# Prompt attention ahead of the mLSTM stages, and layer norms from running sums with raw rows in the up projection, in a one-core decoder layer

## The chip, the cores and the metric

The kernel runs on one core of a Trainium2 chip. The metric is the device time of one execution in microseconds (us), smaller is better. The engines are TensorE (PE), VectorE (DVE), ScalarE (ACT), GpSimd (POOL) and SyncE (SP), which here only issues transfers. Each runs its own program in order, and they meet through semaphores.

## The reference

One step of a hybrid decoder layer for 512 prompt tokens and 8 sequences of 4 sample tokens (544 columns, float32, width 1024):

```python
z = x @ w_in + b_in                      # 27 tiles of 128 features
qk = silu(causal_conv(m_qk)); h = mlstm_chunkwise(...)      # 8 heads of 64
mix_m = sigmoid(m_o) * head_norm(h)
mix_n = g0 * compressed + g1 * selected + g2 * window       # 8 query, 2 kv heads, each softmax + relative bias
x1 = layer_norm(ALPHA * x + concat(mix_m, mix_n) @ w_out, ln1_w, ln1_b)
u = causal_conv(x1 @ w_up + b_up, width 3)                  # 5376 features
y = layer_norm(ALPHA * x1 + (gelu(u[:2688]) * u[2688:]) @ w_down + b_down, ln2_w, ln2_b)
```

Also returned are new cache rows, windows, the mLSTM states and the last rows before each convolution. ALPHA is 2 ** 0.25. `layer_norm` takes mean and variance over the 1024 features of a token.

## The kernel before

Features lie on partitions, tokens in columns: KD = 8 tiles of 128 features and NT = 544 columns (T = 512 prompt, NS = 32 sample). Every dense projection is done in fp32r: weights and activations are each split into a high part (rounded) and a low part (the rest), and three products are summed for each k. `project` (L1653 to L1675) makes one output tile from `parts` weight items: for each k, three products of two matmuls (256 and 288 columns, L1667 and L1669), 48 matmuls for KD = 8.

Weights come as 74 items: 27 of w_in, 8 of w_out (`I_OUT` on), 42 of w_up (`I_UP` on) and 24 of w_down (`I_DOWN` on, 8 tiles in 3 parts of 7 k). SP loads item i into `wring` (4 slots) when item i-4 has been used (`load_weights`, L581 to L585). ACT copies it rounded into `whi` (2 slots) when item i-2 has been used (`split_hi`, L471 to L477; the copy itself is `high`, L466), and DVE makes the low part (`split_lo`, and `low`, L469). `w_hi`, `w_lo` and `w_used` count these steps. All splits stand in the ACT and DVE programs two items ahead of the matmuls.

The stages, in PE's order, all on the same core and with the order written out by hand in each engine's block:

1. In-projection (27 tiles), with the decode attention of the 8 sequences woven into it; then 60 transposes to token rows (L1951), to 308 us.
2. mLSTM for the prompt, four chunks of 128 tokens (PE from L1965), and the sample mLSTM (`sd_*` semaphores), to 412.
3. Pooling of compressed keys and values (L2089, L2090), then the prompt attention: 32 pairs of (block, branch, head) with scores, exponentials, transposes and values, PE two pairs ahead (`PAIRS`, `LAG`), `cmp_scores` and `cmp_transposed` (L2104, L2110) for the compressed branch. ACT and PE wait for `sd_end` 2 and for the copies of state outputs; `mixed` (L1549) writes the upper half of `mixt`.
4. Out projection, 8 tiles from `mixt` (`out_tile`), and with it `norm_pe` and `norm_dve`. After each tile DVE adds ALPHA times the input (L1585, L1588), and PE, in front of the tile after next, adds an average of these rows with a 1/1024 matrix (`average`, L2174 to L2176, two matmuls of float32).
5. Layer norm 1: subtract the mean (L1602, L1605), square on ACT (L989), average the squares on PE, square root (L991, L993), reciprocal of 544 columns (L1608), multiply (L1611), affine on ACT (L996), and splits of x1.
6. Up projection, 42 tiles. For tile n, DVE and ACT run, in this order:

```python
split_lo(dve, I_UP + n + 2)                     # DVE
dve.wait_ge(f_u, n + 1)
link(dve.tensor_scalar(t, u[:, 0:560], ...))    # L1635, first tap
link(dve.scalar_tensor_tensor(out=t, ...))      # L1636, second tap
dve.tensor_copy(fc[:, n, 0:2], u[:, 512:514])   # L1638, and L1639: last rows
dve.scalar_tensor_tensor(out=t, ...).then_inc(f_conv, 1)   # L1640, third tap
# every second tile: gate(n // 2 - 1), gated_lo(n // 2 - 2)

split_hi(act, I_UP + n + 2)                     # ACT
act.activation(us[:, :, 0:2], hf[:, n, :], ACT.Copy)       # L1023
act.activation(u[:, 2:514], q4[n % 2], ACT.Identity, bias=vec("b_up", n))   # L1024, PSUM to SBUF
act.activation(us[:, :, 2:6], ...).then_inc(f_u, 1)        # L1026
# every second tile: gelu(n // 2), gated_hi(n // 2 - 1)
```

   PE may write tile n when `f_u` says that tile n-2 has been read. `gate` (L1627, L1628) multiplies the two halves; `link` orders an operation behind the one before it on the same engine by a semaphore.
7. Down projection, 8 tiles of 3 items (`down_tile`), evicted by ACT into `ybuf` (L1041, L1043), added on DVE (L1597, L1598), averaged as in 4; then layer norm 2 with the same code, and the output.

The SP queue takes, behind the in-projection: the table of biases `relrow` (L611), its shifted form `tb` (L615, 2 MB), the mLSTM states, w_out items 0 to 3, state outputs, the window copy `out_win_s` (L635, 4 MB, memory to memory), the history `hf` of the ffn convolution (L636), the reload of x into `xt` (8 transfers), then all weight items that are left.

## Time and profile before

| | us |
|---|---|
| three runs | 1025.5, 1032.95, 1031.28 |
| median | 1031.28 |
| profiled execution | 1037.76 |
| its span | 1036.1 |
| PE busy | 917.0 (89%) |
| DVE busy | 517.5 (50%) |
| ACT busy | 374.2 (36%) |
| POOL busy | 99.3 (10%) |
| mean granted clock | 0.896 |

The span is the time between the first and the last instruction of one profiled execution, and 1.7 us lie outside it. Busy shares are means over stages that differ. PEclk is the granted clock of TensorE as a share of 2.4 GHz. A matmul that starts while its predecessor runs has a duration that overlaps it; what counts in the projections is the distance from start to start.

### The profile page before, as it was taken

Reading aid. Unit: us, or ns where it says so; the run is one execution under the profiler, and the core shown is the slowest. Engines: PE = TensorE matmul, PEld = TensorE weight load, DVE = VectorE, ACT = ScalarE, POOL = GpSimd, SP = SyncE. Lnnn points to the kernel's source line nnn. Section 1 sums busy time; section 2 is a strip of 40 time slices with the busy share of each in tenths; the row PEclk is TensorE's granted clock in tenths of the full one; section 3 lists DMA queues with packets and bytes.
Section 4 is the critical chain, followed back from the end, with each engine's and each line's share of the span. In section 5 each row is a group of like instructions: output and inputs, shape, how many; then the busy total and the mean of one; then the engine's idle time right before and its main releaser. Section 6 shows DMA issues by size and latency. Waiting matters only on the chain.

```text
span 1036.1 us, 19860 instructions
## 1 busy us (share of the span) xinstructions
PE 917.0 (89%) x7903; PEld 821.8 (79%) x7903; DVE 517.5 (50%) x1116; ACT 374.2 (36%) x742; POOL 99.3 (10%) x164
## 2 busy tenths in 40 slices
PE   5999988998898667888869959999999999999993
PEld 5888877787776553655559839999999999999992
DVE  4522345522335566566752265766776677332325
ACT  4322344644421010345651155434433443222115
POOL 1012213343341002000000000000000000000000
PEclk9989999899896555569989969999999999999997
DMA  8247777676462001400022202222222222222212
GB/s 292 70 145 256 229 264 235 207 223 180 127 233 89 6 1 42 175 1 1 2 87 82 82 1 75 89 82 85 100 82 82 95 90 72 89 90 76 86 33 87
DMA packets 53152, 112.46 MB, mean 109 GB/s; under 512 B 6954, under 2 KB 30283, under 8 KB 52611
## 3 DMA queue, kind: packets, MB, share of 16 engines
q1 hardware_dynamic: 45648, 91.68, 25.9%
q0 software_dynamic: 6528, 17.83, 5.4%
q10 hardware_dynamic: 882, 1.67, 0.5%
q8 instruction: 63, 1.03, 0.4%
q14 instruction: 31, 0.25, 0.1%
HBM read 105.54 MB, written 12.40 MB: 114 GB/s over the span
## 4 chain that ended last, share of the span: by engine, by line
PE 80%; DVE 9%; ACT 4%; issue 3%; DMA 3%; ACTq 0%; POOLq 0%; POOL 0%; SPq 0%; DVEq 0%
PE q L1669 30%; PE q L1667 27%; PE q L2114 3%; DMA arena<-in_pool 2%; PE q L2142 2%; PE q L2132 2%; PE q L1731 1%; PE q L2175 1%; PE q L2176 1%; PE q L2002 1%; PE q L2056 1%; PE q L1719 1%; PE q L1785 1%; ACT whi L956 1%; PE q L1965 1%
## 5 line engine op out<-in xcount | busy, mean ns | idle before, releaser
L469 DVE TENSOR_TENSOR wring_r<-wring,whi_r 128x1024 fp32r<-128x1024 f32 (+1 forms) x101 | 120.5, 1194 | 341.8 <-ACT whi_r L466 341.7
L466 ACT ACTIVATE whi_r<-wring 128x1024 fp32r<-128x1024 f32 (+1 forms) x101 | 104.2, 1033 | 327.8 <-PE q L1669 316.9
L1669 PE MATMUL q<-xt_r,whi_r 128*128 128x288 f32 x552 | 166.9, 302 | 0.0
L1667 PE MATMUL q<-xt_r,whi_r 128*128 128x256 f32 x552 | 157.5, 285 | 0.0
L1667 PE MATMUL q<-arena_r,whi_r 128*128 128x256 f32 x440 | 137.6, 313 | 19.6 <-DVE xt_r L469 11.5
L1669 PE MATMUL q<-arena_r,whi_r 128*128 128x288 f32 x440 | 133.7, 304 | 0.0
L1669 PE MATMUL q<-arena_r,wring_r 128*128 128x288 f32 x440 | 133.0, 302 | 0.0
L1667 PE MATMUL q<-arena_r,wring_r 128*128 128x256 f32 x440 | 125.9, 286 | 0.0
L1667 PE MATMUL q<-mixt_r,whi_r 128*128 128x256 f32 x400 | 113.2, 283 | 10.5 <-DVE xt_r L469 10.5
L1669 PE MATMUL q<-mixt_r,whi_r 128*128 128x288 f32 x400 | 119.4, 298 | 0.0
L1667 PEld LDWEIGHTS q<-arena_r,whi_r 128*128 128x128 f32 x440 | 86.2, 196 | 27.4 <-issue 19.7
L1667 PEld LDWEIGHTS q<-xt_r,whi_r 128*128 128x128 f32 x552 | 107.0, 194 | 0.0
L1669 PEld LDWEIGHTS q<-xt_r,whi_r 128*128 128x128 f32 x552 | 106.8, 193 | 0.0
L1669 PE MATMUL q<-mixt_r,wring_r 128*128 128x288 f32 x336 | 100.1, 298 | 0.0
L1667 PE MATMUL q<-mixt_r,wring_r 128*128 128x256 f32 x336 | 94.5, 281 | 0.0
L1669 PEld LDWEIGHTS q<-arena_r,whi_r 128*128 128x128 f32 x440 | 86.5, 197 | 0.6
L1667 PEld LDWEIGHTS q<-arena_r,wring_r 128*128 128x128 f32 x440 | 85.8, 195 | 0.0
L1669 PEld LDWEIGHTS q<-arena_r,wring_r 128*128 128x128 f32 x440 | 85.4, 194 | 0.0
L1667 PEld LDWEIGHTS q<-mixt_r,whi_r 128*128 128x128 f32 x400 | 76.2, 190 | 11.0 <-issue 10.9
L1669 PEld LDWEIGHTS q<-mixt_r,whi_r 128*128 128x128 f32 x400 | 76.0, 190 | 0.0
L1667 PEld LDWEIGHTS q<-mixt_r,wring_r 128*128 128x128 f32 x336 | 63.6, 189 | 0.0
L1669 PEld LDWEIGHTS q<-mixt_r,wring_r 128*128 128x128 f32 x336 | 63.5, 189 | 0.0
(406 smaller groups left out, 1584.1 us busy)
## 6 DMA issues: line engine op xcount, KB each, us to landing
wring<-in_w_up SPq DMA_DIRECT2D x42, 512.0 KB, 3.2
wring<-in_w_in SPq DMA_DIRECT2D x27, 512.0 KB, 5.1
arena<-in_pool SPq DMA_DIRECT2D x64, 192.0 KB, 3.1
arena<-in_pool POOLq DMA_DIRECT2D x64, 192.0 KB, 3.9
wring<-in_w_down SPq DMA_DIRECT2D x24, 448.0 KB, 3.1
arena<-in_pool SPq DMA_DIRECT2D x64, 64.0 KB, 2.1
arena<-in_pool POOLq DMA_DIRECT2D x64, 64.0 KB, 2.4
wring<-in_w_out SPq DMA_DIRECT2D x8, 512.0 KB, 7.3
```

Of the source, the lines that this page charges most:

```text
L466: return eng.activation(out, src, ACT.Copy)
L469: return eng.tensor_tensor(out, src, hi.bitcast(F32), ALU.subtract)
L956: act.activation(ptb[:, m % 2, g, 0:w], bank[4 + g][:, 0:w], ACT.Copy).then_inc(np_te, 1)
L1667: pe.matmul(out[:, 0, 0:HALF], w, x[:, 0:HALF], start=(kk == 0 and n == 0), stop=(end and n == 2))
L1669: mm = pe.matmul(out[:, 1, 0:HALF + NS], w, x[:, HALF:NT], start=(kk == 0 and n == 0), stop=(end and n == 2))
L1719: mm = pe.transpose(t[:, 128 * k:128 * k + 128], on_chip(g, i, k)[:, 256:384], ident)
L1731: mm = pe.matmul(bank[4][32 * k:32 * k + 32, 128 * s + 64 * e:128 * s + 64 * e + 64], wslide[:, e, h, 12 - 4 * u:44 - 4 * u], pg, start=(i ...
L1785: return pe.matmul(bank[7][ROWS * s:ROWS * s + ROWS, 0:128], probs[:, ROWS * s:ROWS * s + ROWS], v, start=start, stop=stop, skip_group_che ...
L1965: mm = pe.matmul(bank[q], gl[:, token_rows(c)], rows[:, c % 2, 512 * q:512 * q + 512], start=True, stop=True)
L2114: return pe.matmul(bank[6][p, 128 * j:128 * j + 128], v, probs, start=start, stop=stop, skip_group_check=True)
L2132: mm = pe.matmul(bank[2 * (m % 2) + g][:, 0:w], q_of(GQ * g + j, i), zt[64 * g:64 * g + 64, (Z_SK, Z_WK)[k], 0:w], start=True, stop=True)
L2142: mm = pe.transpose(bank[4 + g][:, 128 * kk:128 * kk + 128], pb[:, m % 3, g, 128 * kk:128 * kk + 128], ident)
```

## The change

Two things at once.

Order: the pooling and the prompt attention come directly behind the token transposes, and the mLSTM for the prompt waits for the attention's last block (`np_mx`). Buffers that both used have been moved apart. The first broadcast of the table goes from SP to ACT's queue, at in-projection tile 22; `tb` is loaded in two transfers, columns 384 to 511 first (`tb_in`), the rest (`tb_rest`) awaited by the scores of block 1. The reload of x goes ahead of the sample mLSTM's outputs; `hf` goes ahead of the window copy, and both go ahead of w_out items 4 to 7, at the start of the out projection. The rows of w_out are reordered so that the attention half comes first, and that half of `mixt` is split before the mLSTM ends; behind it DVE makes four low parts, then the low part of w_out item 0.

Norms: in the out projection only tile 0's mean is taken on PE (`first_mean`, inside tile 1), and 8 times it is subtracted from all rows as `shift`. DVE keeps a running `total` of the tiles and a sum of `squares` (squared on ACT). The rows as they are, times ln1_w, are split (`raw_hi` on ACT, `raw_low` on DVE) and go straight into the up projection, with two more columns, ln1_w and ln1_b, in each product (290 columns for 288). Mean and variance are found while it runs: `means` behind k 4 of up tile 0 (averages, and token sums in 5 columns), `variance` and `inverse` on 5 columns, `spread` (back to 544 columns) behind k 2 of tile 1. Each up tile is then corrected from PSUM by DVE (`scaled_rows`), copied by ACT into `u`, and ACT makes the first tap; the copies of the last rows go to POOL. In the down projection DVE rebuilds ALPHA times x1 (`residual`, four or five linked operations) and adds the product from PSUM; `ybuf` is gone, as are the averages behind each tile. The last tile is added to precomputed averages.

```diff
-            sp.wait_ge(rel_out, 16)
-            sp.dma_start(relrow.ap(), relone.ap().unsqueeze(1).broadcast_to([H, 128, NREL])).then_inc(rel_out, 16)
             sp.wait_ge(rel_out, 32)
             sp.wait_ge(nd_mx, GROUPS)
-            shifted = bass.AP(tensor=relrow, offset=127, ap=[[NREL - 1, 128], [128 * NREL, H], [1, 512]])
-            sp.dma_start(tb, shifted).then_inc(tb_in, 16)
+            def shifted_table(first, n):
+                return bass.AP(tensor=relrow, offset=127 + first, ap=[[NREL - 1, 128], [128 * NREL, H], [1, n]])
+            sp.dma_start(tb[:, :, 384:512], shifted_table(384, 128)).then_inc(tb_in, 16)
+            sp.dma_start(tb[:, :, 0:384], shifted_table(0, 384)).then_inc(tb_rest, 16)
             sp.dma_start(ctv, a["ct"]).then_inc(sd_in, 16)
             sp.dma_start(ntv, a["nt"]).then_inc(sd_in, 16)
             sp.wait_ge(w_used, ZT)
-            sp.dma_start(n0, a["n0"]).then_inc(sd_in, 16)
             for i in range(I_OUT, I_OUT + RING):
                 load_weights(i)
+            sp.wait_ge(np_mx, QT)
+            sp.dma_start(n0, a["n0"]).then_inc(sd_in, 16)
             sp.wait_ge(ml_ce, QT)
             sp.dma_start(a["out_c_p"], carried[:, QT % 2]).then_inc(st_cp, 16)
+            sp.wait_ge(ml_mx, 4)
...
             sp.wait_ge(sd_end, 2)
             sp.wait_ge(st_cs, 16)
+            sp.dma_start(hf, a["hf"]).then_inc(hist, 16)
             sp.wait_ge(stored, 64)
             sp.dma_start(a["out_win_s"], a["win"][:, TS:, :]).then_inc(stored, 16)
-            sp.dma_start(hf, a["hf"]).then_inc(hist, 16)
-            sp.wait_ge(np_mx, QT)
-            for k in range(KD):
-                sp.dma_start(xt[:, k, :], a["xt"][:, k, :]).then_inc(xin2, 16)
             for i in range(I_OUT + RING, len(ITEMS)):
...
+            for n in range(UP):
+                pool.wait_ge(f_u, n + 1)
+                pool.tensor_copy(fc[:, n, 0:2], uf[:, n % 4, 512:514])
+                pool.tensor_copy(fc[:, n, 2:18].rearrange("p (b t) -> p b t", b=NB),
+                                 by_sequence(uf, n, 6)[:, :, 4:6]).then_inc(f_last, 1)
...
+                    act.wait_ge(f_last, n - 3)
...
+                act.wait_ge(rw_u, n + 1)
+                act.activation(u[:, 2:514], t[:, 0:T], ACT.Identity, bias=b, scale=-1.0)
+                act.activation(us[:, :, 2:6], t[:, T:NT].rearrange("p (b t) -> p b t", b=NB), ACT.Identity,
+                               bias=b, scale=-1.0).then_inc(f_u, 1)
+                act.wait_ge(f_u, n + 1)
+                act.activation(tf[:, n % 4, 0:560], u[:, 0:560], ACT.Identity, bias=vec("fconv_b", n),
+                               scale=vec("fconv_w", n)).then_inc(f_one, 1)
...
+            def residual(base, m):
+                t = xt[:, m, :]
+                if base == 0:
+                    if m == 0:
+                        dve.wait_ge(xin2, 16 * KD)
+                    else:
+                        link(dve.scalar_tensor_tensor(out=t, in0=t, scalar=ALPHA, in1=shift, op0=ALU.mult, op1=ALU.subtract))
+                else:
+                    link(dve.tensor_tensor(t, raw_lo[:, m, 0:NT].bitcast(F32), raw_hi[:, m, 0:NT].bitcast(F32), ALU.add))
+                    link(dve.tensor_tensor(t, t, rstd, ALU.mult))
+                    link(dve.scalar_tensor_tensor(out=t, in0=mean, scalar=vec("ln1_w", m), in1=t, op0=ALU.mult,
+                                                  op1=ALU.subtract))
+                    link(dve.tensor_scalar(t, t, -ALPHA, var[:, m:m + 1], ALU.mult, ALU.add))
+                    if m >= 1:
+                        link(dve.tensor_tensor(t, t, shift, ALU.subtract))
+            def added(base, m):
+                dve.wait_ge(w_used, I_OUT + m + 1 if base == 0 else I_DOWN + DOWN_PARTS * (m + 1))
+                t = xt[:, m, :]
+                t2, p = t[:, 0:T].rearrange("p (c t) -> p c t", c=2), q4[m % 2]
+                if base == 0 and m == 0:
+                    dve.scalar_tensor_tensor(out=t2, in0=t2, scalar=ALPHA, in1=p[:, :, 0:HALF], op0=ALU.mult, op1=ALU.add)
+                    dve.scalar_tensor_tensor(out=t[:, T:NT], in0=t[:, T:NT], scalar=ALPHA, in1=p[:, 1, HALF:HALF + NS],
+                                             op0=ALU.mult, op1=ALU.add).then_inc(ln_d, 1)
+                else:
+                    dve.tensor_tensor(t2, t2, p[:, :, 0:HALF], ALU.add)
+                    dve.tensor_tensor(t[:, T:NT], t[:, T:NT], p[:, 1, HALF:HALF + NS], ALU.add).then_inc(ln_d, 1)
+            def first_shifted(base):
+                dve.wait_ge(ln_act, act_stat(base // KD, "shift"))
+                dve.wait_ge(ln_d, unshifted(base // KD))
+                dve.tensor_tensor(xt[:, 0, :], xt[:, 0, :], shift, ALU.subtract).then_inc(ln_d, 1)
+                dve.wait_ge(ln_d, shifted_rows(base // KD, 0))
+            def sums(base, m):
+                dve.wait_ge(ln_d, shifted_rows(base // KD, m))
+                link(dve.tensor_tensor(total, total, xt[:, m, :], ALU.add))
+            def sums_of_squares(base, m):
+                dve.wait_ge(ln_q, base + m + 1)
+                dve.tensor_tensor(squares, squares, sq_m, ALU.add).then_inc(ln_a, 1)
+                dve.wait_ge(ln_a, (KD - 1) * (base // KD) + m)
+            def raw_low(m):
+                dve.wait_ge(rw_hi, m + 1 if m == 0 else m + 2)
+                dve.scalar_tensor_tensor(out=raw_lo[:, m, 0:NT], in0=xt[:, m, :], scalar=vec("ln1_w", m),
+                                         in1=raw_hi[:, m, 0:NT].bitcast(F32), op0=ALU.mult,
+                                         op1=ALU.subtract).then_inc(rw_lo, 1)
...
+                residual(0, m)
+                added(0, m)
+                split_lo(dve, I_OUT + m + 2)
                 if m >= 1:
+                    sums(0, m)
+                    sums_of_squares(0, m)
+                    raw_low(m)
...
+            def scaled_rows(n):
+                p, t = q4[n % 2], scaled[n % 2]
+                dve.wait_ge(w_used, I_UP + n + 1)
+                if n == 0:
+                    dve.wait_ge(ln_act, act_stat(0, "copied"))
+                if n >= 2:
+                    dve.wait_ge(f_u, n - 1)
+                c1 = p[:, 1, HALF + NS:HALF + NS + 1]
+                dve.tensor_scalar(rowsum[:, n % 2:n % 2 + 1], p[:, 1, HALF + NS + 1:HALF + NS + 2], vec("b_up", n), None,
+                                  ALU.add)
+                dve.scalar_tensor_tensor(out=t[:, 0:T].rearrange("p (c t) -> p c t", c=2),
+                                         in0=mean[:, 0:T].rearrange("p (c t) -> p c t", c=2), scalar=c1,
+                                         in1=p[:, :, 0:HALF], op0=ALU.mult, op1=ALU.subtract)
+                link(dve.scalar_tensor_tensor(out=t[:, T:NT], in0=mean[:, T:NT], scalar=c1,
+                                              in1=p[:, 1, HALF:HALF + NS], op0=ALU.mult, op1=ALU.subtract))
+                dve.tensor_tensor(t, t, rstd, ALU.mult).then_inc(rw_u, 1)
             for n in range(UP):
+                if n == 0:
+                    variance(0)
+                    inverse(0)
                 split_lo(dve, I_UP + n + 2)
-                dve.wait_ge(f_u, n + 1)
+                scaled_rows(n)
+                dve.wait_ge(f_one, n + 1)
                 u, t = uf[:, n % 4, :], tf[:, n % 4, 0:560]
-                link(dve.tensor_scalar(t, u[:, 0:560], vec("fconv_w", n), vec("fconv_b", n), ALU.mult, ALU.add))
                 link(dve.scalar_tensor_tensor(out=t, in0=u[:, 1:561], scalar=vec("fconv_w", UP + n),
                                               in1=t, op0=ALU.mult, op1=ALU.add))
-                dve.tensor_copy(fc[:, n, 0:2], u[:, 512:514])
-                dve.tensor_copy(fc[:, n, 2:18].rearrange("p (b t) -> p b t", b=NB), by_sequence(uf, n, 6)[:, :, 4:6])
                 dve.scalar_tensor_tensor(out=t, in0=u[:, 2:562], scalar=vec("fconv_w", 2 * UP + n),
                                          in1=t, op0=ALU.mult, op1=ALU.add).then_inc(f_conv, 1)
...
+            dve.wait_ge(ln_pe, pe_stat(1, "mean"))
+            centred(0)
+            variance(1)
+            centred(1)
+            inverse(1)
+            for m in range(2, KD):
+                centred(m)
+            dve.wait_ge(ln_pe, pe_stat(1, "spread"))
+            for m in range(KD):
...
+            def first_mean(n):
+                pe.wait_ge(ln_d, unshifted(n))
+                average(xt[:, 0, :], q4[2]).then_inc(ln_pe, 1)
...
+            def means():
+                pe.wait_ge(ln_a, KD - 1)
+                token_means(total, bank[6])
+                average(total, q4[2]).then_inc(ln_pe, 1)
+                token_means(squares, bank[7]).then_inc(ln_pe, 1)
+            def spread(n):
+                pe.wait_ge(ln_dve, 2 * n + 2)
+                pe.matmul(bank[6], ones, scaled[0][:, 0:T], start=True, stop=True)
+                pe.matmul(bank[7][:, 0:NS], ones, scaled[0][:, T:NT], start=True, stop=True).then_inc(ln_pe, 1)
...
+            pe.wait_ge(sd_end, 2)
+            for m in range(KD):
+                out_tile(m)
             for n in range(UP):
-                if n >= 2:
+                if n < 2:
+                    pe.wait_ge(ln_d, shifted_rows(0, KD - 2 + n))
+                else:
                     pe.wait_ge(f_u, n - 1)
-                project(q4[n % 2], I_UP + n, 1, by_k(x1_hi), by_k(xt_lo), KD, y_lo if n == 0 else None)
-            norm_pe(KD, down_tile)
+                project(q4[n % 2], I_UP + n, 1, by_k(raw_hi), by_k(raw_lo), KD, rw_lo if n == 0 else None,
+                        {0: [(4, means, ())], 1: [(2, spread, (0,))]}.get(n, ()), NT + 2)
+            for m in range(KD):
+                down_tile(m)
+            pe.wait_ge(ln_a, 2 * KD - 3)
+            average(total, q4[2], last=False)
+            token_means(total, bank[6], last=False)
+            token_means(squares, bank[7], last=False)
+            pe.wait_ge(ln_d, shifted_rows(1, KD - 1))
+            average(xt[:, KD - 1, :], q4[2], first=False).then_inc(ln_pe, 1)
+            token_means(xt[:, KD - 1, :], bank[6], first=False)
+            pe.wait_ge(ln_q, 2 * KD)
+            token_means(sq_m, bank[7], first=False).then_inc(ln_pe, 1)
+            spread(1)
```

## Rows read from the trace of the kernel before

**Rows 1.** The page, chain that ended last: share of the span by engine.

```profile
PE 80%; DVE 9%; ACT 4%; issue 3%; DMA 3%; ACTq 0%; POOLq 0%; POOL 0%; SPq 0%; DVEq 0%
PE q L1669 30%; PE q L1667 27%; PE q L2114 3%; DMA arena<-in_pool 2%; PE q L2142 2%; PE q L2132 2%; PE q L1731 1%; PE q L2175 1%; PE q L2176 1%; PE q L2002 1%; PE q L2056 1%; PE q L1719 1%; PE q L1785 1%; ACT whi L956 1%; PE q L1965 1%
```

**Rows 2.** Windows: us, busy PE, PEld, DVE, ACT, POOL, PEclk, DMA share, GB/s.

```profile
308.60:412.50 103.90, 75.77 (x503) 57.00 (x505) 62.31 (x120) 9.71 (x12) 11.43 (x9) 0.55 0.10 39
...
412.50:462.00 49.50, 43.16 (x246) 29.94 (x246) 26.71 (x141) 20.08 (x84) 0.00 (x0) 0.53 0.25 101
462.00:532.10 70.10, 57.98 (x517) 38.05 (x515) 45.27 (x159) 42.85 (x120) 0.00 (x0) 0.97 0.00 1
...
536.40:592.00 55.60, 55.60 (x408) 54.66 (x409) 17.73 (x28) 9.54 (x11) 0.00 (x0) 0.96 0.27 93
592.00:619.20 27.20, 12.88 (x43) 8.34 (x41) 17.10 (x30) 13.54 (x20) 0.00 (x0) 0.76 0.06 20
619.20:875.00 255.80, 255.80 (x2018) 255.69 (x2019) 172.63 (x312) 107.61 (x213) 0.00 (x0) 0.99 0.25 84
875.00:1007.00 132.00, 132.00 (x1032) 131.05 (x1031) 39.05 (x46) 29.70 (x43) 0.00 (x0) 1.00 0.24 77
1007.00:1036.10 29.10, 11.90 (x42) 7.96 (x41) 15.84 (x27) 14.22 (x21) 0.00 (x0) 0.76 0.20 78
```

**Rows 3.** Timeline, PE at the attention's start: start, us, operation, [idle before <-releaser].

```profile
421.95 0.48 PE L2110 MATMUL q<-cst,xt 128*128 128x128 f32 x1 [2.60 <-DVE xt L1522]
```

**Rows 4.** Timeline, PE from the last out tile to the first up tile.

```profile
592.01 0.59 PE L2175 MATMUL q<-xt,cst 128*128 128x256 f32 x2
...
595.33 0.91 PE L2175 MATMUL q<-xt,cst 128*128 128x256 f32 x2 [2.24 <-DVE xt L1588]
...
619.19 0.55 PE L1667 MATMUL q<-mixt_r,whi_r 128*128 128x256 f32 x1 [10.51 <-DVE xt_r L469]
```

**Rows 5.** Timeline, ACT's weight splits: one in out, one in up.

```profile
564.64 1.06 ACT L466 ACTIVATE whi_r<-wring 128x1024 fp32r<-128x1024 f32 x1 [5.85 <-PE q L1669]
...
627.44 1.06 ACT L466 ACTIVATE whi_r<-wring 128x1024 fp32r<-128x1024 f32 x1 [1.96 <-PE q L1669]
```

**Rows 6.** Timeline of SP's queue, and transfers: count, KB each, us to landing.

```profile
414.89 0.77 SPq L635 DMA_DIRECT2D out_win_s<-in_win  x1
...
smem<-in_hf SPq DMA_DIRECT2D x1, 336.0 KB, 22.5
...
wring<-in_w_out SPq DMA_DIRECT2D x8, 512.0 KB, 7.3
...
wring<-in_w_up SPq DMA_DIRECT2D x42, 512.0 KB, 3.2
```

**Rows 7.** Timeline, DVE in one up tile with a gate.

```profile
797.62 1.23 DVE L469 TENSOR_TENSOR wring_r<-wring,whi_r 128x1024 fp32r<-128x1024 f32 x1 [2.50 <-ACT whi_r L466]
798.77 0.57 DVE L1635 TENSOR_SCALAR smem<-zt,col 128x560 f32<-128x560 f32 x1
799.37 0.80 DVE L1636 SCALAR_TENSOR_TENSOR smem<-zt,col,smem 128x560 f32<-128x560 f32 x1
...
801.07 0.68 DVE L1627 TENSOR_TENSOR zt<-smem 128x512 f32<-128x512 f32 x1
...
801.77 0.72 DVE L469 TENSOR_TENSOR zt_r<-zt,arena_r 128x544 fp32r<-128x544 f32 x1
```

**Rows 8.** Timeline, ACT in one up tile.

```profile
791.56 0.67 ACT L1024 ACTIVATE zt<-q,col 128x512 f32<-128x512 f32 x1
792.13 0.28 ACT L1026 ACTIVATE zt<-q,col 128x32 f32<-128x32 f32 x1
792.30 0.67 ACT L1011 ACTIVATE smem<-smem 128x560 f32<-128x560 f32 x1
```

**Rows 9.** Groups by form: ACT's affine of the norms (busy, mean ns, idle).

```profile
L996 ACT ACTIVATE xt<-xt,col 128x544 f32<-128x544 f32 x16 | 12.6, 827 | 8.8 <-DVE xt L1611 8.8
```

**Rows 10.** Timeline, the second norm's reciprocal and affine.

```profile
1023.00 3.55 DVE L1608 RECIPROCAL smem<-smem 128x544 f32<-128x544 f32 x1 [6.42 <-ACT smem L993]
...
1027.35 5.96 ACT L996 ACTIVATE xt<-xt,col 128x544 f32<-128x544 f32 x8 [4.38 <-DVE xt L1611]
```

More of the change, by code:

```diff
@@ L227, in layer @@
         xt, zt, wring, whi_f, mixt, arena = (sb(*t) for t in large("", F32))
+        raw_lo, work = xt_r, xt[:, :, :].rearrange("p k c -> p (k c)")
+        xt_r, xt = (t[:, :, 0:NT] for t in (xt_r, xt))
         cst = sb("cst", [128, NC128])
@@ new lines, in gated @@
+            def gated(m):
+                i, k, j, slot = m // 8, m // 4 % 2, m % 4, m % 3
+                dve.wait_ge(np_e, NG * m + 2)
+                link(dve.reciprocal(dens[:, 4 + slot, :], dens[:, slot, :]))
+                for g in range(NG):
+                    v, gate = pb[:, slot, g, 0:128 * i + 128], 104 + 24 * i + 8 * k + GQ * g + j
+                    dve.tensor_scalar(v, v, dens[:, 4 + slot, g:g + 1], gcol[:, gate:gate + 1],
+                                      ALU.mult, ALU.mult).then_inc(np_p, 1)
@@ L1306, in _ @@
+            mixed(QT - 1)
             rescale = s4[:, 16:32]
```

679 lines of the change are left out of this document (360 added, 319 removed).

## The prediction

> **What bounds the kernel now.** I read the chain of waits first: TensorE holds 80% of it, and two matmul lines alone 57% [rows 1]. The windows by stage come next [rows 2]. The reader is to see three kinds of stage in them. In the out, up and down projections PE is busy for the whole stretch (55.6, 255.8 and 132 us). In the two layer norms (592 to 619.2 and 1007 to 1036.1) it is busy for 12.9 and 11.9 us of 27.2 and 29.1. In mLSTM and prompt attention no engine is full, and the clock is 0.55 and 0.53 until 462, so a hand-over chain sets the pace. The change touches all three. The first norm is nearly pure delay, and it goes; but its work goes to the up stage, where DVE is busy for 172.6 of 255.8 us, or 4.11 us of each 6.09 us tile. So the question is what VectorE and ScalarE need per tile afterwards.
>
> The sum is made against the profiled execution, 1037.76 us (span 1036.1 and 1.7 around it); it is 6.5 us above the median of 1031.28, which I take off again at the end. Less than 1% (10 us) can't be told from no change here.
>
> **Swap of attention and mLSTM: -2.** Both stages stand in series before and after, with the same instructions, and only the first sees another state of the clock. The stretches of 103.9 and of 119.6 us (49.5 and 70.1) are laid in the other order [rows 2]. The attention waits for its table of biases, but columns 384 to 511, all that block 0 reads, are loaded ahead of the other three quarters, and those are wanted at block 1 only. So no wait shows there. The gain could be in the clock: the first 49.5 us of attention run at 0.53 (1.2 GHz), with DVE busy for 26.7 (54%), against 65% (45.27 of 70.1) later at 0.97. At that share they would take 26.7/0.65 = 41, 8 us less. But attention has a hole of 2.60 us just behind its start [rows 3], and a hole of 2.24 us in the norm was followed by matmuls at half speed (0.91 us per pair against 0.59) [rows 4]. I take -2, with bounds of -10 (the clock stays up, and mLSTM's start gets some of it too) and +3 (mLSTM's first 10 us slower). Splitting the attention half of the mix early leaves 3.9 us between the last mLSTM product and the first out tile, about the 4.3 of before.
>
> **Out projection: -4.3, +1.5.** Before, one average of 0.87 us stands behind each tile, so a weight split of 1.06 comes after 5.85 idle, every 6.91 us [rows 5], instead of 6.04. Now it is 8 x 6.04 + 2.1 slow start + 0.87 for the one first average = 51.3, against 55.6. DVE has two more 544-column additions, a subtraction and a raw low part: 1.14 + 0.7 + 4 x 0.72 = 4.8 us a tile, which TensorE's 6.04 hides (if it were not hidden: nothing up to 6.04, then 1 for 1).
> The 4 MB window copy now goes into SP's queue ahead of w_out tiles 4 to 7, and every load behind it waits. Before it was issued 3 us after the mLSTM stage, and what was queued behind it took 22.5 us to land [rows 6]. Now: 3 + 0.8 + 22.5 = 26.3, then a weight tile, 3.2 us if it is like the up loads, 7.3 like the out loads: tile 4 lands at 29.5 to 33.6. TensorE would start it at 3.9 + 2.1 + 0.87 + 4 x 6.04 = 31.0, and the two splits before that take 2.3, so it is late from 28.7 on, by 0.8 to 4.9. I take +1.5, since the copy will have the queues for itself; bounds 0 and 7.1 (4.9 and a slow restart of 2.2: the first up tile took 8.2 us from 619.19 to 627.44 for 6.01 [rows 4, 5]).
>
> **First norm: -27.2.** Raw rows split behind each out tile are ready when the last tile ends: for the last of them, product 7 of the first up tile, the low part comes 4.5 us after it and is wanted after 7 x 0.75 = 5.3. The hole of 2.24, the average and the 3.55 us reciprocal on 544 columns go from the path. The whole 27.2 us window goes [rows 2]. Bounds -27.2 and -25 (the row sum late once).
>
> **Up projection: +41.4.** TensorE's own time stays near 6.04 (290 columns for 288, under 0.02 each) plus the token means, 2.8, and spread, 0.95, in the first two tiles: 260.5. But VectorE is now in a round trip with ScalarE inside each tile. One iteration, in its program order, from rows of DVE and ACT in one old tile [rows 7, 8]:
> - weight low part: 1.14 to the next start (797.62 to 798.77).
> - row sum 0.08, scaled residual 0.60 (801.07 to 801.77 holds the same pair, 512 and 32 columns, as 0.60 and 0.10), 32 columns 0.21, times rstd 0.73: 1.62.
> - ACT's copy into u 0.57, the 32 columns 0.28, then the first tap with scale and bias. The trace has no 560-column one; for 544 with a scale and bias column it shows 827 ns [rows 9], for 560 without them 0.67. I take 0.85. With three hand-overs of 0.03: 1.79. In all of it VectorE stands, as every later operation of its program, gates and low parts too, waits behind this one; ScalarE's next weight split stands behind its wait for the scaled rows.
> - two taps: 0.84 + 0.71 (799.37 and its partner; linked steps start 0.03 after the end of the one before, free ones 0.08 before it).
> Sum 6.10. Even tiles add a gate and a low part, 1.33 (801.07 to the end of 801.77), so 7.43. After odd ones ScalarE does gelu, gated high part and weight split (0.58 + 0.57 + 1.06 less overlap = 2.15) while VectorE is ready after 1.58: +0.57. A pair is 6.10 + 7.43 + 0.57 = 14.1, 7.05 a tile against 6.04. VectorE's first u comes at 15.7; 15.7 + 20 x 14.1 = 297.7, so the stage is about 297.2: +41.4. TensorE gets holes of about 0.65 and 1.4 us per pair. Bounds: a tap of 0.67 gives 290 (+34); ScalarE never late gives 13.53 a pair, 286 (+30); links that cost nothing, 0.6 less a tile, 272 (+16); at 7.3 a tile 308 (+52). The copies of the last columns to POOL cost nothing: POOL has none busy in this stage [rows 2], and what waits on them is four tiles on.
> The Trainium skill speaks for a shorter cycle: "VectorE: DVE Perf Modes", section "The DRAIN you can't avoid", says that a semaphore between two operations costs nothing extra. The rows here differ: linked operations stand 0.12 us later than free ones. By the rule the stage would take the 272 of the last bound.
>
> **Down projection: +4.** Seven averages go (7 x 0.87 = 6.1, of which 5.2 lie in the stage) and one comes: -4.4. But VectorE ends the up stage late: after the last tile's taps it has a gate, two low parts, the prelude of the norm and a five-link residual before the third split. From the stage's start: 3.9 for what is left of tile 40 (taps, gate, low part), 6.1 for tile 41, 1.3 for the last gelu and gate, 1.4 for two low parts, 1.0 for the prelude, 3.2 for the residual and its links: that split ends at 16.9, and part 2 wants it after two parts of 5.3 (7 x 0.755), at 10.6. So +6.3, with a restart of 2.1 on top of -4.4. 132 becomes 136. Bounds -4.4 and +8.
>
> **Second norm: -6.3.** Averages of 544 columns and the reciprocal (3.55) [rows 10] become five-column ones: last value added 1.0, average 3.7, token sums 5.6, variance, root and inverse 8.3, subtractions 13.1, eight multiplies of 0.7 from PSUM 18.8, last ScalarE affine 19.9, and 2.8 from there to the end as before (1033.3 to 1036.1): 22.7 for 29.05. Bounds -9 and -3.
>
> **Sum.** -2 -4.3 +1.5 -27.2 +41.4 +4 -6.3 = +7.1: 1044.9 for the profiled execution, 1038.4 against the median, 0.7% above it. The gain of 38 us in the norms and averages is given back in the up stage.
>
> **The rivals.**
> (1) The up stage stays bound by TensorE, 260.5, and VectorE isn't late in down: -2 -4.3 +1.5 -27.2 +4.7 -4.4 -6.3 = -38: 993. For it: VectorE's own steps are (14.1 - 0.57 - 2 x 1.79) / 2 = 5.0 us of 6.04. Against it: the 1.79 us round trip stands in its program order, with no second tile's work between. 0.07.
> (2) Smaller: a faster cycle, 6.8 a tile (links or tap cheaper), and the clock up in the first attention: 297.2 - 42 x 0.25 = 286.7, +30.9 instead of +41.4, so 1027.9; with -8 for -2 as well, 1021.9. If links cost nothing at all, it is 272, +16, so 1013: 0.04 of this chance. (That is the time by the rule of the Trainium skill named above.) For: bounds above. Against: the measured links. 0.20.
> (3) Slower: the window copy ahead of w_out tile 4. It decides if that tile lands later than 28.7 us after the mLSTM stage; at 33.6 the price is 4.9 + 2.2 instead of 1.5: 1044.0. For: all out loads before took 7.3. Against: those stood in a crowd of other transfers. 0.15.
> (4) Short holes lower the clock again and again in the up stage. A restart costs 2.2 us [rows 4, 5]; in each of 21 pairs it would be mostly absorbed in the 2.05 us that TensorE has to spare: +4, 1042.5, and more if it never recovers (8.2 a tile: 1086). For it: the hole of 2.24 us. Against it: these holes, 0.65 and 1.4, are shorter than that one. The Trainium skill has a rule for it: "TensorE: Matmul & The Clock Gate", section "A second HAM failure mode: psum-queue depth-cycling", by which frequent short gaps between groups make the clock swing. 0.12.
> (5) Each hand-over is dearer than I take it, 7.3 a tile: +10.5, 1049. 0.12.
> (6) My forecast, 0.34, its own range 1028 to 1048.
>
> **Numbers.** Faster by over 1% (below 1021): (1) and 0.11 of (2) and 0.03 of mine, 0.21. Slower (above 1041.6): (3), (4), most of (5), 0.03 of mine, less 0.06 of them that ends nearer: 0.36. Within: 0.43. The range from 1015 to 1054 leaves out (1), the end of (2) and the tails of (4) and (5), 0.17 in all.
>
> **What would show it.** Up stage of about 297 us with PE busy share near 0.87, DVE intervals of 7.05 a tile, its idle time put down to ACT's first tap; no hole between out and up; out stage near 51 to 53; ACT's tap near 0.85; the tail 23 us behind the last down tile; w_out tile 4 landing near 29.5. Wrong, if DVE idles for TensorE in the up stage (then 993), or if the granted clock there is below 0.95.

## The result, and the profile after

The changed kernel takes 1048.87 us (median of 4 runs, 1048.64 to 1051.07) against 1032.12 for the kernel before (4 runs, 1025.5 to 1033.49): ratio 1.0181, 95% interval 1.0151 to 1.0211. I had forecast 1038.4, 0.7% above the median, which I counted as no change. The time lies inside the range of 1015 to 1054, but the loss is 1.8%, it can be measured, and it is more than twice what was forecast.

The chain that ended last, after:

```profile
PE 50%; DVE 23%; ACT 13%; issue 9%; DMA 3%; POOL 0%; SPq 0%; ACTq 0%; DVEq 0%; POOLq 0%
PE q L1837 15%; PE q L1835 15%; DVE cst L1764 3%; DMA arena<-in_pool 3%; ACT zt L1082 3%; DVE wring_r L493 3%; DVE cst L1759 3%; ACT whi_r L490 2%; PE q L2155 2%; ACT smem L1086 2%; PE q L2173 2%; DVE smem L1774 2%; PE q L2183 2%; PE q L1899 2%; PE q L2262 1%
```

TensorE had 80% of it and the two projection lines 57% [rows 1]; now they have 50% and 30%, and DVE and ACT hold 36% between them, with the lines of the up stage (L1764 times rstd, L1082 copy into u, L1086 first tap, L1774 second tap).

Windows by stage after (us, busy PE, PEld, DVE, ACT, POOL, PEclk, DMA share, GB/s), to be read beside [rows 2]. The stages are attention, mLSTM, out, up, down and the second norm:

```profile
306.60:418.90 112.30, 94.45 (x741) 61.85 (x741) 71.93 (x299) 61.56 (x200) 0.57 (x1) 0.85 0.01 4
418.90:526.40 107.50, 74.88 (x488) 56.59 (x489) 67.58 (x128) 15.62 (x22) 13.79 (x11) 0.56 0.10 35
526.40:577.70 51.30, 51.29 (x389) 51.14 (x390) 36.92 (x56) 17.44 (x26) 0.10 (x1) 0.95 0.42 155
577.70:885.00 307.30, 270.31 (x2046) 260.66 (x2044) 211.74 (x353) 142.77 (x253) 12.80 (x81) 1.00 0.22 72
885.00:1021.65 136.65, 130.08 (x1013) 129.57 (x1014) 75.94 (x108) 31.32 (x40) 0.55 (x4) 0.98 0.24 74
1021.65:1046.80 25.15, 10.31 (x54) 8.74 (x52) 14.01 (x40) 8.40 (x12) 0.00 (x0) 0.59 0.23 89
```

Up is the only stage that got much longer: 307.3 us for 255.8. TensorE is busy in it for 270.3, at a granted clock of 1.00, and DVE for 211.7, which is no full engine either. What it waits for stands in two views of the trace. First PE in two neighbouring tiles, then the waits of PE and of DVE in this stage (waiter, releaser: us in total, times, longest):

```profile
622.35 0.39 PE L1835 MATMUL q<-arena_r,whi_r 128*128 128x256 f32 x1 [0.54 <-ACT zt L1083]
630.07 0.39 PE L1835 MATMUL q<-arena_r,whi_r 128*128 128x256 f32 x1 [1.35 <-ACT zt L1083]
```

```profile
PE q L1835 <- ACT zt L1083: 36.9, 39, 1.4
...
DVE smem L1774 <- ACT smem L1086: 75.7, 40, 1.9
DVE wring_r L493 <- ACT whi_r L490: 10.9, 22, 1.5
```

PE has holes of 0.54 and 1.35 us in each pair of tiles, put down to ACT's copy into u, since that frees the PSUM bank. But ACT itself waits for DVE, and DVE stands 40 times for 1.9 us until ACT's first tap is done. So one chain goes back and forth between the two. One pair of it, on DVE and then on ACT:

```profile
660.13 0.80 DVE L1774 SCALAR_TENSOR_TENSOR smem<-zt,col,smem 128x560 f32<-128x560 f32 x1 [1.89 <-ACT smem L1086]
660.97 0.80 DVE L1776 SCALAR_TENSOR_TENSOR smem<-zt,col,smem 128x560 f32<-128x560 f32 x1
662.19 1.23 DVE L493 TENSOR_TENSOR wring_r<-wring,whi_r 128x1024 fp32r<-128x1024 f32 x1 [0.41 <-ACT whi_r L490]
663.33 0.21 DVE L1757 TENSOR_SCALAR sm<-q,col 128x1 f32<-128x1 f32 x1
663.46 0.74 DVE L1759 SCALAR_TENSOR_TENSOR cst<-dsc,q 128x512 f32<-128x512 f32 x1
664.12 0.24 DVE L1762 SCALAR_TENSOR_TENSOR cst<-dsc,q 128x32 f32<-128x32 f32 x1
664.40 0.72 DVE L1764 TENSOR_TENSOR cst<-cst,dsc 128x544 f32<-128x544 f32 x1
667.02 0.80 DVE L1774 SCALAR_TENSOR_TENSOR smem<-zt,col,smem 128x560 f32<-128x560 f32 x1 [1.89 <-ACT smem L1086]
...
674.73 0.80 DVE L1774 SCALAR_TENSOR_TENSOR smem<-zt,col,smem 128x560 f32<-128x560 f32 x1 [1.89 <-ACT smem L1086]
```

```profile
665.16 0.72 ACT L1082 ACTIVATE zt<-cst,sm 128x512 f32<-128x512 f32 x1 [2.90 <-DVE cst L1764]
665.79 0.31 ACT L1083 ACTIVATE zt<-cst,sm 128x32 f32<-128x32 f32 x1
666.13 0.86 ACT L1086 ACTIVATE smem<-zt,col 128x560 f32<-128x560 f32 x1
```

It is the chain of the prediction, step for step, only longer: 6.89 us from 660.13 to 667.02 and 7.71 to 674.73, 14.60 a pair for the 14.1 forecast.

The stages from first matmul to first matmul, of the two traces:

| stage | before | forecast | after | change |
|---|---|---|---|---|
| in-projection, to the transposes | 300.45 | 0 | 296.64 | -3.8 |
| transposes, attention, mLSTM, splits | 235.9 | -2 | 229.8 | -6.1 |
| out projection and first norm | 82.8 | -30.0 | 51.3 | -31.5 |
| up | 255.6 | +41.4 | 307.3 | +51.7 |
| down | 132.3 | +4 | 136.6 | +4.3 |
| second norm | 29.0 | -6.3 | 25.15 | -3.9 |
| span | 1036.1 | +7.1 | 1046.8 | +10.7 |

The first line is chance: in the eleven traces of this study the transposes start anywhere from 294.0 to 300.45, in either order of the stages, and the first trace of the kernel before is the latest. That is most of why its profiled execution stood 6.5 us above its median, while the changed kernel's (1048.81) lies at its median (1048.87). Taking 6.5 off was right.

### The profile page after: what moved, and what is told of

It reads as the page before. It is cut to its first block, busy times and chain, and to the rows that moved or that the text cites. A ratio compares the mean times of both kernels' runs of the same rounds, so it can differ in the third digit from the quotient of the medians.

```text
span 1046.8 us, 20115 instructions
## 1 busy us (share of the span) xinstructions
PE 901.9 (86%) x7863; PEld 806.2 (77%) x7863; DVE 595.6 (57%) x1233; ACT 400.1 (38%) x767; POOL 112.6 (11%) x248
## 4 chain that ended last, share of the span: by engine, by line
PE 50%; DVE 23%; ACT 13%; issue 9%; DMA 3%; POOL 0%; SPq 0%; ACTq 0%; DVEq 0%; POOLq 0%
PE q L1837 15%; PE q L1835 15%; DVE cst L1764 3%; DMA arena<-in_pool 3%; ACT zt L1082 3%; DVE wring_r L493 3%; DVE cst L1759 3%; ACT whi_r L490 2%; PE q L2155 2%; ACT smem L1086 2%; PE q L2173 2%; DVE smem L1774 2%; PE q L2183 2%; PE q L1899 2%; PE q L2262 1%
## 5 line engine op out<-in xcount | busy, mean ns | idle before, releaser
L1835 PE MATMUL q<-arena_r,whi_r 128*128 128x256 f32 x712 | 216.1, 304 | 62.9 <-ACT zt L1083 36.6
L1837 PE MATMUL q<-arena_r,whi_r 128*128 128x288 f32 (+1 forms) x712 | 214.0, 301 | 0.0
L1837 PE MATMUL q<-arena_r,wring_r 128*128 128x288 f32 (+1 forms) x712 | 213.1, 299 | 0.0
L1835 PE MATMUL q<-arena_r,wring_r 128*128 128x256 f32 x712 | 202.5, 284 | 0.0
L1835 PEld LDWEIGHTS q<-arena_r,whi_r 128*128 128x128 f32 x712 | 137.3, 193 | 78.6 <-ACT zt L1083 45.2
L1837 PE MATMUL q<-xt_r,whi_r 128*128 128x290 f32 (+1 forms) x552 | 165.5, 300 | 0.0
L1837 PEld LDWEIGHTS q<-arena_r,whi_r 128*128 128x128 f32 x712 | 137.7, 193 | 0.1
L1835 PEld LDWEIGHTS q<-arena_r,wring_r 128*128 128x128 f32 x712 | 137.0, 192 | 0.0
L1837 PEld LDWEIGHTS q<-arena_r,wring_r 128*128 128x128 f32 x712 | 136.7, 192 | 0.0
L1082 ACT ACTIVATE zt<-cst,sm 128x512 f32<-128x512 f32 x42 | 30.3, 722 | 159.2 <-DVE cst L1764 159.2
L1774 DVE SCALAR_TENSOR_TENSOR smem<-zt,col,smem 128x560 f32<-128x560 f32 x42 | 33.7, 802 | 79.5 <-ACT smem L1086 79.5
L1837 PE MATMUL q<-zt_r,whi_r 128*128 128x288 f32 x176 | 52.3, 299 | 0.0
L1835 PE MATMUL q<-zt_r,whi_r 128*128 128x256 f32 x176 | 49.4, 282 | 0.0
L965 ACT ACTIVATE xt<-xt 128x128 f32<-128x128 f32 (+3 forms) x64 | 35.4, 554 | 28.2 <-DVE xt L1410 27.8
```

Of the source, the lines that this page charges most:

```text
L965: act.activation(v, v, ACT.Exp, bias=mxs[:, 4 + slot, g:g + 1], accum_out=dens[:, slot, g:g + 1]).then_inc(np_e, 1)
L1082: act.activation(u[:, 2:514], t[:, 0:T], ACT.Identity, bias=b, scale=-1.0)
L1774: link(dve.scalar_tensor_tensor(out=t, in0=u[:, 1:561], scalar=vec("fconv_w", UP + n), in1=t, op0=ALU.mult, op1=ALU.add))
L1835: pe.matmul(out[:, 0, 0:HALF], w, x[:, 0:HALF], start=(kk == 0 and n == 0), stop=(end and n == 2))
L1837: mm = pe.matmul(out[:, 1, 0:width - HALF], w, x[:, HALF:width], start=(kk == 0 and n == 0), stop=(end and n == 2))
```

## The experiments

Theory A: in the up stage VectorE and ScalarE hand each tile back and forth, and what VectorE could do meanwhile stands behind the wait in its program. The rivals are VectorE's work as such, the clock, and the swap.

**The kernel before, again.**

> The kernel before, unchanged, for a second trace. Theory A (the clock of the first 50 us of attention is chance): its profiled execution is not at 1037.8 again but 4 to 12 us shorter, and the difference lies in the attention stage (119.6 us in the first trace) or in the in-projection (300.5 us). Theory B (the order sets the clock): 1035 to 1038 us again, attention at 119 to 120 us with a granted clock of 0.53 in its first 50 us.

Measured, in one run: 1031.88 us, span 1030.2, so 5.9 us less than the first trace's 1036.1. PE, start of the transposes and of the out projection:

```profile
295.62 6.63 PE L1951 MATMUL q<-cst,zt 128*128 128x128 f32 x54 [1.20 <-DVE zt L1081]
...
530.39 0.55 PE L1667 MATMUL q<-arena_r,whi_r 128*128 128x256 f32 x1 [4.28 <-DVE mixt_r L469]
```

The transposes start 4.8 us earlier, so most of the difference is in the in-projection. From transposes to out it is 234.8 us, against 235.9 in the first trace, and the first 49 us of attention have a granted clock of 0.57, against 0.53: attention is about as slow again. Theory A was right of the place it named second, B of the attention.

**The swap alone.**

```diff
# the kernel before, with the changed kernel's order of the stages, its buffers,
# its transfers (table, x, hf, window copy) and the early split of the mix; old norms
-            pe.wait_ge(np_mx, QT)
+            pe.wait_ge(sd_end, 2)
             norm_pe(0, out_tile)
```

> Only the swap of attention and mLSTM, with the buffers, queues and early splits that go with it; the norms, the up and the down projection stay as before. Theory B (the order keeps the clock up in attention, and the table's transfer is out of the in-projection's way): the -10 us that the trace of the changed kernel shows between the start and the out projection is real, so ratio 0.990, about 1022. Theory A (the first trace of before was a slow one in these stages): the ratio is 0.996 to 1.0, about 1029 to 1032, and the changed kernel's loss of 17 us against the median is the norms' alone.

Measured: 1030.59 us (12 runs) against 1031.24 (23 runs), ratio 0.9999 (0.9982 to 1.0016). From transposes to out its trace has 232.15 us, 2.6 less than the second trace of before, while the out projection and its norm take 0.2 and the second norm 0.5 more. So the swap is worth at most 2 us (the interval is -1.9 to +1.6 us), no more than what was forecast (-2), and the loss belongs to the norms. The 229.8 of the changed kernel's trace is at the low end: this trace and six others with the new order have 231.2 to 232.2, one has 229.2.

**The first tap back on VectorE.**

```diff
-                act.wait_ge(f_u, n + 1)
-                act.activation(tf[:, n % 4, 0:560], u[:, 0:560], ACT.Identity, bias=vec("fconv_b", n),
-                               scale=vec("fconv_w", n)).then_inc(f_one, 1)
...
-                dve.wait_ge(f_one, n + 1)
+                dve.wait_ge(f_u, n + 1)
+                link(dve.tensor_scalar(t, u[:, 0:560], vec("fconv_w", n), vec("fconv_b", n), ALU.mult, ALU.add))
```

> The changed kernel with the first convolution tap back on VectorE, behind f_u. Theory A (the round trip sets the up stage): VectorE stands only for 1.0 us (0.03 + 0.63 + 0.31 + 0.03) instead of 1.89, and does 0.60 more itself; ScalarE is no longer late after odd tiles. 6.1 and 7.45 a tile for 6.89 and 7.71, so a pair takes 13.5 for 14.6: the up stage takes 284 for 307, the whole 1026. Theory B (VectorE's work as such sets it, the stand is hidden by something): VectorE has 42 x 0.6 = 25 us more work, and the whole gets 10 to 25 us longer, 1059 to 1074.

Measured: 1029.7 us, ratio 0.9983 (0.9964 to 1.0002), 19 us less than the changed kernel. The up stage is 286.2 us (284 expected), with more work on VectorE, 233.2 us busy for 211.7:

```profile
581.50:867.70 286.20, 265.60 (x2045) 260.31 (x2044) 233.19 (x394) 110.60 (x212) 24.21 (x82) 1.00 0.24 77
```

```profile
664.56 0.57 DVE L1771 TENSOR_SCALAR smem<-zt,col 128x560 f32<-128x560 f32 x1 [1.00 <-ACT zt L1083]
```

The stand is 1.00 for 1.89. More work on the engine in the chain, and a shorter time: it is the round trip that costs, not the work. Theory B falls.

**The weight low part behind the scaled rows.**

```diff
-                split_lo(dve, I_UP + n + 2)
+                if n == 0:
+                    split_lo(dve, I_UP + n + 2)
                 scaled_rows(n)
+                if n >= 1:
+                    split_lo(dve, I_UP + n + 2)
                 dve.wait_ge(f_one, n + 1)
```

> The changed kernel with the weight low part of tile n+2 moved from ahead of the scaled rows of tile n to behind them (from tile 1 on): the same instructions, another order on VectorE. Theory A (the stand in the round trip is the cost): the low part of 1.14 lies in the 1.89 us stand, VectorE needs 1.79 + 1.89 + 1.55 = 5.2 in odd and 6.6 in even tiles, 5.9 on average, and TensorE's 6.04 sets the stage: 262 us for 307, the whole 1004, below the kernel before. Theory B (the sum of VectorE's work and hand-overs, whatever the order): no change, 1046 to 1050. Theory C (short holes throttle the clock): the stage stays above 280 with a granted clock below 0.95.

Measured: 1000.75 us, ratio 0.9702 (0.9675 to 0.973). The up stage takes 260.2 us. Its window, with nearly the same busy time on VectorE, then VectorE in one tile:

```profile
581.00:841.00 260.00, 259.93 (x2044) 259.07 (x2043) 213.55 (x356) 147.91 (x253) 13.04 (x82) 1.00 0.26 85
```

```profile
665.89 0.73 DVE L1764 TENSOR_TENSOR cst<-cst,dsc 128x544 f32<-128x544 f32 x1
666.53 1.22 DVE L493 TENSOR_TENSOR wring_r<-wring,whi_r 128x1024 fp32r<-128x1024 f32 x1
668.51 0.80 DVE L1777 SCALAR_TENSOR_TENSOR smem<-zt,col,smem 128x560 f32<-128x560 f32 x1 [0.76 <-ACT smem L1086]
```

The low part lies in the stand, which shrinks from 1.89 to 0.76, and PE is busy for 259.9 of 260.0 us. The down stage takes 132.3 us for 136.6, since VectorE comes less late to it: TensorE's hole in down tile 0, 6.57 us in the changed kernel, is 2.62 us here. This is one instruction in another place of the program, with the same work on each engine, and it is worth 48 us. It makes the change a gain.

**Half of it.**

```diff
-                split_lo(dve, I_UP + n + 2)
+                if n % 2 == 0:
+                    split_lo(dve, I_UP + n + 2)
                 scaled_rows(n)
+                if n % 2 == 1:
+                    split_lo(dve, I_UP + n + 2)
```

> The changed kernel with the weight low part behind the scaled rows in odd tiles only, half of the order that took the whole loss away. Theory A (the cycle of VectorE and ScalarE sets the stage until TensorE does): the 1.14 us go from one of the two tiles of a pair, 14.61 becomes 13.47, the up stage 283 for 307 and the whole 1025. Theory B (it is a matter of either or: one late tile in a pair keeps the stage at its old pace): 300 us or more in the up stage, 1040 or more.

Measured: 1026.14 us, ratio 0.9965 (0.9941 to 0.9988); the up stage 284.8 us for 283 expected. Half of the edit gives 22.5 of its 47.1 us, as in a chain that nothing else bounds yet.

**Two links more.**

```diff
-                dve.tensor_scalar(rowsum[:, n % 2:n % 2 + 1], ...)
-                dve.scalar_tensor_tensor(out=t[:, 0:T], ...)
+                link(dve.tensor_scalar(rowsum[:, n % 2:n % 2 + 1], ...))
+                link(dve.scalar_tensor_tensor(out=t[:, 0:T], ...))
```

> The changed kernel with two links more in each tile's scaled rows on VectorE: the row sum and the 512-column step are each waited for before the next step starts, which nothing needs. Theory A (a link between two VectorE operations costs 0.12 us on the engine that sets the stage, as linked steps start 0.03 to 0.04 behind the end and free ones 0.08 before it): 42 x 2 x 0.12 = 10 us more, 1059. Theory B (a semaphore between two VectorE operations costs nothing, the rule of the Trainium skill that was weighed in the prediction): no change, 1047 to 1051.

Measured: 1062.59 us, ratio 1.0317 (1.0292 to 1.0342). The up stage takes 317.7 us, 10.4 more than 307.3; 10.4 / 84 = 0.12 us a link. DVE, the row sum and the step behind it:

```profile
677.55 0.21 DVE L1757 TENSOR_SCALAR sm<-q,col 128x1 f32<-128x1 f32 x1
677.80 0.75 DVE L1759 SCALAR_TENSOR_TENSOR cst<-dsc,q 128x512 f32<-128x512 f32 x1
```

The distance is 0.25 for the 0.13 of 663.33 to 663.46. The other 3 to 4 us of the whole lie ahead of the up stage (it starts at 581.4 for 577.7), in the parts that vary. So a semaphore between two VectorE steps isn't free where that engine is in the chain. The Trainium skill's rule from the prediction ("VectorE: DVE Perf Modes", section "The DRAIN you can't avoid"), which it took from eight tensor copies, doesn't hold for these steps: the measurement is 0.12 us a link. The same section of the Trainium skill says that a next operation that is not held starts earlier, and there the trace agrees: in the changed kernel, without the link, the 512-column step starts 0.08 us before the recorded end of the row sum.

**Other operands.**

```diff
-                c1 = p[:, 1, HALF + NS:HALF + NS + 1]
+                c1 = vec("ln1_w", 0)
...
-                act.activation(u[:, 2:514], t[:, 0:T], ACT.Identity, bias=b, scale=-1.0)
+                act.activation(u[:, 2:514], t[:, 0:T], ACT.Identity, bias=b)
```

> The changed kernel with two operands changed, so that part of the computation is left out: the scaled rows take their factor from a constant column in SBUF and not from the product's own column in PSUM, and ScalarE's copy into u goes without the scale of -1. It measures what made the two steps longer than forecast. If the PSUM factor costs, the 512-column step of VectorE takes 0.68 (as the 512-column steps of before) and not 0.74; if the scale costs, ScalarE's copy takes 0.67 and not 0.72. If neither, both stay, and it is the source (two tensors from different memories on VectorE, SBUF in place of PSUM on ScalarE) that makes them longer.

Measured, in one run: 1049.8 us, up stage 307.0. Groups by form of the changed kernel, then of this one (busy, mean ns):

```profile
L1759 DVE SCALAR_TENSOR_TENSOR cst<-dsc,q 128x512 f32<-128x512 f32 x42 | 31.2, 742 | 0.0
...
L1082 ACT ACTIVATE zt<-cst,sm 128x512 f32<-128x512 f32 x42 | 30.3, 722 | 159.2 <-DVE cst L1764 159.2
```

```profile
L1759 DVE SCALAR_TENSOR_TENSOR cst<-dsc,col,q 128x512 f32<-128x512 f32 x42 | 31.0, 737 | 0.0
...
L1082 ACT ACTIVATE zt<-cst,sm 128x512 f32<-128x512 f32 x42 | 30.3, 723 | 158.8 <-DVE cst L1764 158.8
```

Neither the place of the factor (PSUM or SBUF) nor ScalarE's scale makes the steps longer than the rows that they were estimated from. For VectorE the traces show what does: that the factor is a column, one value for each partition, wherever it lies. The kernel before has the same kind of step with a constant as factor (ALPHA), and it too reads one tensor in SBUF and one in PSUM; the changed kernel has both kinds with all tensors in SBUF. First two groups of the kernel before, with the constant, then two of the changed kernel, with the constant and with a column:

```profile
L1585 DVE SCALAR_TENSOR_TENSOR xt<-xt,q 128x512 f32<-128x512 f32 x8 | 5.4, 680 | 0.0
L1588 DVE SCALAR_TENSOR_TENSOR xt<-xt,q 128x32 f32<-128x32 f32 x8 | 1.4, 180 | 0.0
```

```profile
L1657 DVE SCALAR_TENSOR_TENSOR xt<-xt,smem 128x544 f32<-128x544 f32 x7 | 5.0, 719 | 0.0
L1661 DVE SCALAR_TENSOR_TENSOR xt<-dsc,col,xt 128x544 f32<-128x544 f32 x8 | 6.3, 785 | 0.3
```

With a column 512 columns take 742 ns for 680, 32 columns 244 (L1762) for 180, and 544 columns 785 for 719: 62 to 66 ns more at each size. In this run, too, the factor was a column, so it could not show this. For ScalarE, what is left is where its source lies (it reads SBUF now, where it read PSUM); no run tried that by itself.

**The residual behind the low part, at the start of down.**

```diff
+                if m >= 1:
+                    residual(KD, m)
-                residual(KD, m)
                 for c in range(DOWN_PARTS):
                     i = I_DOWN + DOWN_PARTS * m + c
                     if i + 2 < len(ITEMS):
                         split_lo(dve, i + 2)
+                    if m == 0 and c == 0:
+                        residual(KD, m)
```

> The changed kernel with tile 0's residual of the down projection behind the low part of part 2 on VectorE, not ahead of it: the same instructions. Theory A (TensorE's hole of 6.57 us in down tile 0 is VectorE's lag from the up stage, the residual's 2.9 us among it): part 2 starts 2.9 us earlier, the stage takes 133.7 us for 136.6, the whole 1046 for 1049. Theory B (that hole is the w_down tile's transfer or ScalarE's high part): no change, 136.6.

Measured: 1048.9 us (6 runs from 1045.87 to 1053.2), ratio 1.018 (1.0149 to 1.0212): no difference that the timed runs can show, as 3 us are less than that spread, so the whole time leaves it open. The trace does not. PE at part 2 of down tile 0, in the changed kernel and in this one:

```profile
902.32 0.58 PE L1835 MATMUL q<-arena_r,whi_r 128*128 128x256 f32 x1 [6.57 <-DVE wring_r L493]
```

```profile
899.90 0.39 PE L1838 MATMUL q<-arena_r,whi_r 128*128 128x256 f32 x1 [3.71 <-DVE wring_r L493]
```

The hole is 2.86 us shorter, and the stage takes 133.4 us for 136.6. Behind the hole of 6.57 the clock is at its lower level from the first matmul on (0.58). Behind that of 3.71 the first four matmuls are at the upper level, and then it falls too, 0.6 us later:

```profile
900.71 0.44 PE L1840 MATMUL q<-arena_r,wring_r 128*128 128x288 f32 x1
```

This kind takes 0.30 at full clock. The matmuls are slow from 900.5 to 903.9 here, and from 902.3 to 906.6 in the changed kernel.

**Four subtractions ahead of the variance.**

```diff
-            centred(0)
+            for m in range(4):
+                centred(m)
             variance(1)
-            centred(1)
+            centred(4)
             inverse(1)
-            for m in range(2, KD):
+            for m in range(5, KD):
                 centred(m)
```

> The version with the low part behind the scaled rows, and in the second norm four subtractions ahead of the variance's first step, not one. Behind the last down tile VectorE stands for 3.0 us for the token sums while seven subtractions wait behind it. If VectorE's own work sets the tail, as the trace says, these 3 us are filled and the tail is 22 us for 24.8, the whole 998. If the chain over the token sums, root and spread sets it, nothing changes: 1000 to 1001.

Measured: 996.67 us (5 runs), ratio 0.9664 (0.9633 to 0.9695), the fastest version of the study. The second norm takes 22.43 us for 24.8. VectorE at the variance's first step, in the changed kernel and in this one:

```profile
1029.72 0.17 DVE L1705 COPY var<-q 128x5 f32<-128x5 f32 x1 [3.02 <-PE q L2350]
```

```profile
982.14 0.16 DVE L1705 COPY var<-q 128x5 f32<-128x5 f32 x1 [0.16 <-PE q L2354]
```

Against the version without this edit (1000.75, 4 runs at another time) the 4 us are more than the 2.4 of the trace, and the runs of each spread over 4 to 8 us; the trace's 2.4 is the safer figure.

## Why the prediction was wrong

By its own steps:

- **Swap, -2.** Right as far as the runs can tell: -0.1 us in the timed comparison, with an interval of -1.9 to +1.6, and -2.6 in the trace of the swap alone. The hole behind attention's start is still there (1.97 us), and the granted clock, 1.00 until 309.3, is 0.50 from this hole on, as forecast.
- **Out projection, -4.3 and +1.5.** The first is exact (51.3). The second was not needed. The split of w_out item 4 on ACT:

```profile
549.33 1.06 ACT L490 ACTIVATE whi_r<-wring 128x1024 fp32r<-128x1024 f32 x1 [3.74 <-DMA wring<-in_w_out]
```

  ACT waited 3.74 us for that transfer, but it landed 26.7 us behind the last mLSTM row (522.6), where I had it at 29.5 to 33.6 and the limit at 28.7. TensorE never noticed. Rival (3) is out, by 2 us: the right side of its condition, but with little to spare.
- **First norm, -27.2.** Right: the up stage starts without a hole.
- **Up, +41.4.** This is the step that failed, in size alone: it measured +51.7. The mechanism was right in each part, but the pair of tiles is 14.6 us, not 14.1, and 21 pairs make 10 us of it. The scaled rows take 1.79 for 1.62 (row sum 0.13 for 0.08, the 512 columns 0.66 for 0.60, the 32 columns with their link 0.28 for 0.21, rstd 0.72 for 0.73). The round trip takes 1.90 for 1.79 (copy into u 0.63 for 0.57, 32 columns and link 0.34 for 0.31, tap 0.86 for 0.85, the rest in hand-overs). Only ScalarE's lateness came shorter, 0.50 for 0.57. The biggest part was a misread row: I priced the scaled residual with the pair of 801.07 [rows 7] as "the same pair", but that is a plain product of two tensors, and the new steps take a factor from a column, which costs VectorE 62 to 64 ns in each of the two. The copy into u was priced with one that read PSUM. No row of before stood behind the 0.08 of the row sum. So nearly all of the errors had one sign, times 42. Rival (5), with a chance of 0.12, gave the time that came, 7.3 us a tile and 1049, but not for its reason: the hand-overs between the engines cost 0.03 to 0.04 us, for the 0.03 that I had counted, and it is the steps that were longer.
- **Down, +4.** Right (+4.3), and its cause shown: 2.86 us of the hole are the residual, and the hole shrinks from 6.57 to 2.62 us when VectorE isn't late from the up stage. What is left of it still ends with VectorE's low part and is followed by a stretch at the lower clock, so that stage takes 132.3 us, as before, though the seven averages are gone from it.
- **Second norm, -6.3.** It gave 3.9. The term that was too small is the token sums, 1.9 us from the average to their end (3.7 to 5.6): they took 3.8 (1025.9 to 1029.7), with a granted clock of 0.53 in this stretch. Ten of these matmuls with one column take 2.27 us there, where twenty took 2.29 at a clock of 1.00, just ahead of it (from 1022.56). The average came 0.6 later than forecast and the end 0.3, the variance took 0.4 less; subtractions (4.8) and multiplies (5.7) were right. With four subtractions ahead of the variance the stage takes 22.43 us, near the 22.7 of the forecast, but by another way: the token sums are as slow there, and VectorE works in their shadow, which the forecast had not counted.
- **Rival (1)** (TensorE-bound, 993) was false for this kernel, but names what one edit makes of it: 1000.75. **Rival (4)** (clock): false. The up stage has a hole in each tile, 0.54 and 1.35 us, and its granted clock is 1.00. By the rule of the Trainium skill ("TensorE: Matmul & The Clock Gate", section "A second HAM failure mode: psum-queue depth-cycling") frequent short gaps make the clock swing; the trace does not show that for these holes.
- **The faster cycle of rival (2)**: false; links cost what the rows of before said.

The sum of steps was +7.1 on the profiled execution, and the two traces differ by +10.7: up adds 10.3 to the forecast, the second norm 2.4, down 0.3; the out projection gives back 1.5, the stages between the transposes and out 4.1, and the in-projection, by chance, 3.8. On the medians, where that chance is out, 1048.87 stands against the 1038.4 of the forecast, 10.5 more, which is about what the up stage alone was short by. The chances were drawn too low on the slow side for the same reason: the bounds of the up term (+30 to +52) were set as if it could err both ways alike, and +51.7 is at their end.

## What to carry to other kernels

When work moves to an engine that is "half idle", count the loop's hand-overs in its own program order, not its busy share: VectorE was busy for 212 of 307 us and set the stage. Where such a wait can't be avoided, put work that nobody waits for behind the request and ahead of the wait; here one moved instruction turned a loss of 1.8% into a gain of 3.0%. And for a term that repeats 42 times, price each step with its link and with a row of the same kind of step, a factor from a column included; here the errors were nearly all on the long side.
